# Late conditioning sections in a two-layer diffusion backbone: half of each one scaled by ScalarE and added up by GpSimd during the attention

## The chip, the cores and the metric

The kernel runs on one core of a Trainium2 chip. The core has TensorE (matmuls), VectorE, ScalarE and GpSimd (elementwise work), a sync engine whose queue issues transfers, and 16 DMA engines. The metric is the device time of one execution in microseconds, lower is better. All data are float32; a float32 matmul stands in the profile as two matmul instructions.

## The reference

Two layers over 512 latent tokens of width 1024, with 256 context tokens. Each layer takes six conditioning sections of width 1024 (shift, scale and gate, twice) out of one vector:

```
m = silu(c) @ ada_w[l] + ada_b[l]
sh1, sc1, g1, sh2, sc2, g2 = split(m, 6)
h  = rms_norm(x) * (1 + sc1) + sh1
x  = x + g1 * mixer(h)          # layer 0: pooling groups and 8 attention heads; layer 1: Conformer convolution
h2 = rms_norm(x) * (1 + sc2) + sh2
x  = x + g2 * experts(h2)       # 16 experts, each takes 64 tokens
```

`ada_w[l]` is 1024 x 6144: a section is a product of the vector with 1024 x 1024 weights, 4 MB. The context tokens have a conditioning vector of their own (`c_ctx`), which only the first two sections of layer 0 need. In the attention each head scores 512 queries against 768 keys (context and latents), takes a softmax, and weighs the values.

## The kernel before

Weights stream through `ring`, six slots of 2 MB (`SLOTS`), in the order of `ORDER`. Granule number g lies in slot g % 6 and is loaded once the granule six places before it is used up (`slot_free`, L497). All these loads are issued in program order by the sync engine (SP), so a load that waits holds back the ones behind it.

The program has these stages: the first four conditioning sections, input projection and pooling (`L0`); the attention, head by head; the output projection and the routing to experts; the experts of layer 0 (`mixture`, eight pairs); the convolution; the experts of layer 1. In the expert stages 2 MB granules follow each other through the same six slots. The first of them, besides two that lie ready in the ring, waits for the last head's output (`spare_free`, `o_done`).

Sections 4 to 9 are the six late ones (`LATE`). Head h of the attention (h = 0 to 5) computes section h + 4. Each section is loaded in two halves b = 0, 1 of 1024 x 512. A half lies in a slot as 8 pieces of 128 x 512, one for each k, and the vector as `cond`, 8 columns of 128. `ada_block` multiplies the pieces with `cond` in matmuls with 32 columns of weights; columns 0 to 15 hold copies of the latents' vector and 16 to 31 of the context's. Four row groups of the result hold four partial sums; ScalarE copies them to `ada_rows` (`late_rows_out`), TensorE transposes them (`late_turn`), and VectorE adds the four (`section_sum`, `section_bias`).

In one head the engines work as follows (tile qt = 0 to 3 stands for 128 queries):

- TensorE (L954): transposes of the last head's tile 2, late block b = 0, scores of tiles 0 and 1, transposes of tile 3, late block b = 1, scores of tile 2, the last head's product with the values (L931), transposes of tile 0, the first late turn, scores of tile 3, the second late turn, transposes of tile 1, the next head's queries (`project_queries`, L890), and after odd heads the next two heads' keys (L898).
- ScalarE (L1297): for each tile exp of the scores (L1305). Copies of the late rows (L1295) stand ahead of the exps of tile 0 and behind that of tile 1, the head's output (L1289) behind that of tile 2, the next queries (L1274) at the end.
- VectorE (L1686): for each tile the maximum of the scores (L1695), the bias from it, the division by the sum of the tile before (L1681, L1683), a copy of transposed tiles (L1675). The late sums stand at tile 3, and the next queries wait for the second of them (`section_summed`).
- GpSimd stages the next heads' weights (`stage_two_heads`).
- SP issues the load of half b of section h + 1 when late block b of head h is done (L628, L633). The two halves have one slot each.

Of the kernel before, what the change touches and what calls it, by code (L numbers as in the profile page):

```python
# [18 lines left out]
N = 512  # L19
# [5 lines left out]
HEADS = 8  # L25
# [185 lines left out]
def drains(engine, through):  # L211
# [12 lines left out]
         + [("ada", b) for b in range(4, 2 * EARLY)] + [("late", 0), ("late", 1), ("mixout", 0), ("mixout", 1)]  # L224
# [15 lines left out]
G_LATE = GRANULE[("late", 0)]  # L240
TWO_DMAS = set()


def arrivals(g):

    return 16 * sum(LATE if ORDER[n][0] == "late" else 1 + (n in TWO_DMAS) for n in range(g % SLOTS, g + 1, SLOTS))

# [24 lines left out]
def build(nc, x_in, c_in, ctx_in, cctx_in, ada_w, ada_b, norm1_g, norm2_g, mix_w_in, pool_w, pool_scale,  # L272
# [7 lines left out]
    with stack:  # L280
# [159 lines left out]
        edges_in, pads_set, pooled = map(sem, ("edges_in", "pads_set", "pooled"))  # L440
        cond_in, consts_in, params_in, small_in, attn_w_in = map(
# [50 lines left out]
        def _(sp):  # L492
# [4 lines left out]
            def slot_free(g):  # L497
# [4 lines left out]
                elif ORDER[before][0] == "moe1":  # L502
                    sp.wait_ge(moe_used, MOE_GRANULES + ORDER[before][1] + 1)
                elif ORDER[before][0] == "late":
                    sp.wait_ge(late_filled, 2 * LATE)
                else:
                    sp.wait_ge(filled, last_use(before) + 1)
# [17 lines left out]

            def late_slot(b):
                return slot(G_LATE + b).rearrange("p (k n) -> p k n", k=K8)

# [33 lines left out]
            for b in range(2):  # L562
                slot_free(G_LATE + b)
                sp.dma_start(late_slot(b), ada_blocks(0)[EARLY, b, :, :, :]).then_inc(slot_in[(G_LATE + b) % SLOTS], 16)
# [61 lines left out]
            for b in range(2):  # L626
                sp.wait_ge(late_filled, b + 1)
                sp.dma_start(late_slot(b), ada_blocks(0)[EARLY + 1, b, :, :, :])\  # L628
                  .then_inc(slot_in[(G_LATE + b) % SLOTS], 16)
            with sp.Fori(0, LATE - 2, 1) as s:  # L630
                for b in range(2):
                    sp.wait_ge(late_filled, 2 * s + (b + 3))
                    sp.dma_start(late_slot(b), ada_blocks(1)[s, b, :, :, :])\  # L633
                      .then_inc(slot_in[(G_LATE + b) % SLOTS], 16)
# [41 lines left out]
        def _(pe):  # L676
# [259 lines left out]
            def late_block(h, b):  # L936

                g = G_LATE + b
                pe.wait_ge(slot_in[g % SLOTS], arrivals(g) - 16 * (LATE - 1) + 16 * h)
                if b == 0:  # L940
                    pe.wait_ge(q_nope_done, h + 1)
                    pe.wait_ge(q_rope_done, h + 1)
                else:
# [1012 lines left out]
```

## Time and profile before

| | |
|---|---|
| median of 3 runs | 1548.9 us (1544.6 to 1551.72) |
| profiled execution | 1544.04 us, its span 1542.1 us |
| TensorE matmuls | 1418.3 us busy, 92% |
| VectorE, ScalarE, GpSimd | 432.8, 230.2, 70.9 us busy |
| DMA | 500.08 MB, mean 324 GB/s |
| mean granted TensorE clock | 0.984 |

The span runs from the first to the last instruction of one profiled execution. In the slices a digit is a tenth of busy time in 1/40 of the span (38.6 us). The attention lies from about 126 to 280 us, slices 4 to 8. The chain of waits follows the work back from the last instruction; whatever isn't on it could be longer without a change of the end, up to a point.

### The profile page before, as it was taken

The numbers are of one execution on the slowest core, as the hardware profiler recorded it, in microseconds if no ns is written. First come the engines' busy times: TensorE is split into PE (matmuls) and PEld (weight loads), VectorE is DVE, ScalarE is ACT, GpSimd is POOL, SyncE is SP. The second block draws the span as 40 slices with busy tenths as digits, with TensorE's granted clock in tenths as the row PEclk, the third lists the DMA queues.
The fourth block names the chain that finished last, engine by engine and source line by source line (L and its number), as shares of the span: only waits on it lengthen the run. The fifth ranks groups of instructions, "written<-read, shape, count | busy, mean of one in ns | idle before, by whom it ended". The sixth has DMA issues, their size and how long they took to land.

```text
span 1542.1 us, 15155 instructions
## 1 busy us (share of the span) xinstructions
PE 1418.3 (92%) x5813; PEld 586.7 (38%) x5813; DVE 432.8 (28%) x884; ACT 230.2 (15%) x469; POOL 70.9 (5%) x155
## 2 busy tenths in 40 slices
PE   5999999988999989899989999997999898999996
PEld 3544555443333332332324444453433333323322
DVE  2234667341111121111214323524012211111113
ACT  3223333111010100010003112121101000100001
POOL 1001000000000000000000300001000000000001
PEclk9999999999999999999999999998999999999999
DMA  9736683259999999999999004229999999999995
GB/s 358 263 134 235 227 300 154 82 222 382 426 400 428 427 428 428 427 428 428 421 419 365 5 0 164 95 90 348 429 415 412 428 428 428 428 429 428 423 421 218
DMA packets 77233, 500.08 MB, mean 324 GB/s; under 512 B 7752, under 2 KB 8799, under 8 KB 48766
## 3 DMA queue, kind: packets, MB, share of 16 engines
q1 hardware_dynamic: 71502, 484.10, 76.9%
q0 software_dynamic: 2304, 8.39, 1.4%
q10 hardware_dynamic: 3376, 6.86, 1.2%
q8 instruction: 38, 0.62, 0.2%
q14 instruction: 13, 0.11, 0.0%
HBM read 493.03 MB, written 6.31 MB: 324 GB/s over the span
## 4 chain that ended last, share of the span: by engine, by line
PE 66%; DMA 25%; DVE 5%; issue 1%; SPq 1%; ACT 1%; POOL 0%; POOLq 0%; DVEq 0%; ACTq 0%
PE PS L1039 28%; DMA ring<-in_exp_wg_dram 11%; DMA ring<-in_exp_wu_dram 9%; PE PS L837 7%; PE PS L1071 5%; PE PS L710 4%; PE PS L868 4%; DMA ring<-in_exp_wd_dram 3%; PE PS L681 3%; PE PS L910 3%; PE PS L693 2%; PE PS L766 2%; PE PS L762 2%; PE PS L931 1%; PE PS L852 1%
## 5 line engine op out<-in xcount | busy, mean ns | idle before, releaser
L1039 PE MATMUL PS<-ring,arena 128*64 128x512 f32 x2880 | 666.7, 601 | 43.3 <-DMA ring<-in_exp_wg_dram 19.1
L1039 PEld LDWEIGHTS PS<-ring,arena 128*64 128x64 f32 x2880 | 220.7, 138 | 458.1 <-issue 417.2
L1741 DVE TENSOR_TENSOR x<-x,PS 128x512 f32<-128x512 f32 x128 | 87.9, 687 | 465.7 <-PE PS L1071 465.7
L1071 PE MATMUL PS<-arena 128*128 128x512 f32 x256 | 141.5, 641 | 3.7 <-DVE arena L1768 3.2
L837 PE MATMUL PS<-ring,hT 128*128 128x512 f32 x256 | 113.9, 600 | 0.0
L1352 ACT ACTIVATE arena<-PS 128x512 f32<-128x512 f32 x32 | 17.4, 594 | 462.3 <-PE PS L1039 462.3
L1768 DVE SCALAR_TENSOR_TENSOR arena<-PS,arena,g_row 128x512 f32<-128x512 f32 x32 | 22.5, 746 | 218.3 <-PE PS L1039 218.3
L1071 PEld LDWEIGHTS PS<-arena 128*128 128x128 f32 x256 | 38.3, 188 | 105.1 <-issue 96.9
L681 PE MATMUL PS<-ident,arena 128*128 128x128 f32 (+4 forms) x393 | 54.1, 277 | 21.9 <-DVE arena L1759 18.0
L837 PEld LDWEIGHTS PS<-ring,hT 128*128 128x128 f32 x256 | 48.7, 192 | 59.8 <-issue 59.1
L1354 ACT ACTIVATE arena<-PS 128x512 f32<-128x512 f32 x16 | 9.6, 597 | 340.8 <-PE PS L681 340.8
L681 PEld LDWEIGHTS PS<-ident,arena 128*128 128x128 f32 (+4 forms) x393 | 44.4, 159 | 39.1 <-DVE arena L1759 22.3
L710 PE MATMUL PS<-ring,hT 128*128 128x512 f32 x128 | 56.7, 594 | 1.1 <-ACT hT L1289 1.1
L868 PE MATMUL PS<-ring,hT 128*128 128x512 f32 x128 | 56.4, 594 | 0.0
L693 PE MATMUL PS<-ring,cond 128*32 128x512 f32 x384 | 49.3, 642 | 2.1 <-DMA ring<-in_ada_w_dram 1.3
L681 PE MATMUL PS<-ident,xn 128*128 128x128 f32 x212 | 30.7, 291 | 15.2 <-DVE xn L1389 13.7
L1873 POOL DMA_INDIRECT xn<-xn_rows,token_at x16 | 15.3, 959 | 554.9 <-PE PS L681 516.6
L681 PEld LDWEIGHTS PS<-ident,xn 128*128 128x128 f32 x212 | 28.6, 188 | 29.1 <-issue 24.5
L1695 DVE TENSOR_REDUCE arena<-PS 128x1 f32<-128x768 f32 x32 | 30.6, 956 | 28.6 <-PE PS L910 27.4
L1305 ACT ACTIVATE arena<-PS,arena 128x768 f32<-128x768 f32 x32 | 28.9, 902 | 62.0 <-PE PS L681 33.3
L1128 ACT ACTIVATE xn<-x 128x1024 f32<-128x1024 f32 x20 | 21.1, 1057 | 108.6 <-DVE x L1422 60.2
L1759 DVE TENSOR_TENSOR arena<-arena,PS 128x512 f32<-128x512 f32 x32 | 20.4, 680 | 57.0 <-PE PS L1039 57.0
(183 smaller groups left out, 1077.6 us busy)
## 6 DMA issues: line engine op xcount, KB each, us to landing
ring<-in_exp_wg_dram SPq DMA_DIRECT2D x62, 2048.0 KB, 16.0
ring<-in_exp_wd_dram SPq DMA_DIRECT2D x62, 2048.0 KB, 19.8
ring<-in_exp_wu_dram SPq DMA_DIRECT2D x56, 2048.0 KB, 17.8
ring<-in_ada_w_dram SPq DMA_DIRECT2D x24, 2048.0 KB, 10.1
ring<-in_conv_w_pw_dram SPq DMA_DIRECT2D x6, 2048.0 KB, 19.6
hT<-in_exp_wu_dram SPq DMA_DIRECT2D x4, 2048.0 KB, 15.2
ring<-in_mix_w_out_dram SPq DMA_DIRECT2D x2, 2048.0 KB, 18.9
arena<-in_exp_wu_dram SPq DMA_DIRECT2D x2, 2048.0 KB, 7.8
```

Of the source, the lines that this page charges most:

```text
L681: return nc.tensor.transpose(o, i, ident[0:rows, 0:rows])
L693: last = nc.tensor.matmul(PS[r:r + 32, bank, :], cond[:, k, :], w[:, k, :], start=k < 4, stop=k >= 4)
L710: last = nc.tensor.matmul(PS[:, bank_of(n)[0], :], catT[:, k, t * 128:(t + 1) * 128], w, start=k == 0, stop=k == K8 - 1)
L762: last = nc.tensor.matmul(B, w, hT[:, k, :], start=k == 0, stop=k == K8 - 1)
L766: last = nc.tensor.matmul(B[:, 0:b - a], h, w, start=k == 0, stop=k == K8 - 1)
L837: last = nc.tensor.matmul(B, hT[:, k, t * 128:(t + 1) * 128], w[:, k, :], start=k == 0, stop=k == K8 - 1)
L868: last = nc.tensor.matmul(B, hT[:, k, t * 128:(t + 1) * 128], w, start=k == 0, stop=k == K8 - 1)
L910: last = nc.tensor.matmul(S[qt % 2][:, a:b], qT[:, qt * 128:(qt + 1) * 128], keys[odd][:, a:b], start=True, stop=True)
L1039: last = nc.tensor.matmul(PS[64 * e:64 * e + 64, bank + half, :], lhs[:, k, 64 * e:64 * e + 64], w[e][:, half * N:(half + 1) * N], start=k ...
L1071: nc.tensor.matmul(PS[:, 6 + i % 2, :], hot[:, (i // 2) * 128:(i // 2 + 1) * 128], y_rows[:, (i % 2) * N:(i % 2 + 1) * N], start=True, sto ...
L1695: v.reduce_max(maxima[:, qt:qt + 1], S[qt % 2][:, 0:768], AX.X).then_inc(max_step, 1)
L1741: v.tensor_tensor(part, part, PS[:, 6 + i % 2, :], ALU.add).then_inc(scat_added, 1)
```

## The change

Half b = 1 of a late section is no longer multiplied by TensorE. ScalarE multiplies each of its 8 pieces by the vector's column for that k, in place in the ring slot (`scale_late`), two pieces behind each exp of the head before; the pieces of section 4 are scaled before the first queries. GpSimd adds the 8 pieces up in 7 steps into `ada_rows[:, 1]` (`add_late`), between the stagings. The same late turns transpose the rows, and VectorE adds over all 128 partitions' values (`section_total`, 512 values in and 4 out, where `section_sum` took 32 in and 8 out). So that this sum is right for the half that TensorE computes too, `cond` is cleared and holds each vector in one column only, and the context's column is cleared before the attention.

Half b = 1 now has two slots that take turns (granules late 1 and late 2), half b = 0 has one. All loads of late sections stand in one loop, half 0 ahead of half 1 for each section. Half 0 of section number h waits for late block h - 1, half 1 for the sum of section h - 2. The granules behind them move by one slot. The loops over heads of ScalarE and GpSimd are written out.

```
-         + [("ada", b) for b in range(4, 2 * EARLY)] + [("late", 0), ("late", 1), ("mixout", 0), ("mixout", 1)]
+         + [("ada", b) for b in range(4, 2 * EARLY)] + [("late", 0), ("late", 1), ("late", 2), ("mixout", 0), ("mixout", 1)]
...
+LATE_STEPS = K8 - 1
...
+LATE_LOADS = (LATE, LATE // 2, LATE // 2)
...
-    return 16 * sum(LATE if ORDER[n][0] == "late" else 1 + (n in TWO_DMAS) for n in range(g % SLOTS, g + 1, SLOTS))
+    return 16 * sum(LATE_LOADS[ORDER[n][1]] if ORDER[n][0] == "late" else 1 + (n in TWO_DMAS) for n in range(g % SLOTS, g + 1, SLOTS))
...
+        cond_cleared, late_cond, late_scaled, late_sum = map(sem, ("cond_cleared", "late_cond", "late_scaled", "late_sum"))
...
+                elif ORDER[before] == ("late", 0):
+                    sp.wait_ge(late_filled, LATE)
...
-                    sp.wait_ge(late_filled, 2 * LATE)
+                    sp.wait_ge(late_sum, LATE_STEPS * (LATE - 2 + ORDER[before][1]))
...
-            def late_slot(b):
-                return slot(G_LATE + b).rearrange("p (k n) -> p k n", k=K8)
...
-            for b in range(2):
-                slot_free(G_LATE + b)
-                sp.dma_start(late_slot(b), ada_blocks(0)[EARLY, b, :, :, :]).then_inc(slot_in[(G_LATE + b) % SLOTS], 16)
...
-            for b in range(2):
-                sp.wait_ge(late_filled, b + 1)
-                sp.dma_start(late_slot(b), ada_blocks(0)[EARLY + 1, b, :, :, :])\
-                  .then_inc(slot_in[(G_LATE + b) % SLOTS], 16)
-            with sp.Fori(0, LATE - 2, 1) as s:
+            for h in range(LATE):
                 for b in range(2):
-                    sp.wait_ge(late_filled, 2 * s + (b + 3))
-                    sp.dma_start(late_slot(b), ada_blocks(1)[s, b, :, :, :])\
-                      .then_inc(slot_in[(G_LATE + b) % SLOTS], 16)
+                    g = G_LATE + b * (1 + h % 2)
+                    if h < 1 + b:
+                        slot_free(g)
+                    elif b:
+                        sp.wait_ge(late_sum, LATE_STEPS * (h - 1))
+                    else:
+                        sp.wait_ge(late_filled, h)
+                    l, s = divmod(EARLY + h, SECTIONS // 2)
+                    sp.dma_start(slot(g).rearrange("p (k n) -> p k n", k=K8), ada_blocks(l)[s, b, :, :, :])\
+                      .then_inc(slot_in[g % SLOTS], 16)
...
-            def late_block(h, b):
-                g = G_LATE + b
+            def late_block(h):
+                g = G_LATE
                 pe.wait_ge(slot_in[g % SLOTS], arrivals(g) - 16 * (LATE - 1) + 16 * h)
-                if b == 0:
-                    pe.wait_ge(q_nope_done, h + 1)
-                    pe.wait_ge(q_rope_done, h + 1)
-                else:
-                    pe.wait_ge(late_rows, 2 * h + 1)
+                pe.wait_ge(late_cond, 1)
+                pe.wait_ge(q_nope_done, h + 1)
+                pe.wait_ge(q_rope_done, h + 1)
...
-                    pe.wait_ge(late_rows, 2 * h + 2)
+                    pe.wait_ge(late_rows, h + 1)
+                    pe.wait_ge(late_sum, LATE_STEPS * h + LATE_STEPS)
...
             def head(h, odd, first, more, late):
...
-                    late_block(h, 0)
+                    late_block(h)
...
-                if late:
-                    late_block(h, 1)
...
+            act_e.wait_ge(cond_cleared, 1)
...
-                sc.activation(cond[:, :, 16 * v:16 * v + 16], cond_raw[:, v, :].unsqueeze(2).to_broadcast([128, K8, 16]),
-                              ACT.Silu).then_inc(cond_ready, 1)
+                sc.activation(cond[:, :, 16 * v:16 * v + 1], cond_raw[:, v, :].unsqueeze(2), ACT.Silu).then_inc(cond_ready, 1)
...
-            def late_rows_out(h, b):
-                act_e.wait_ge(late_filled, 2 * h + b + 1)
-                sc.activation(ada_rows[:, b, :], PS[:, 7, :], ACT.Copy).then_inc(late_rows, 1)
-            def head(j, odd, first, more, late):
+            def late_rows_out(h):
+                act_e.wait_ge(late_filled, h + 1)
+                sc.activation(ada_rows[:, 0, :], PS[:, 7, :], ACT.Copy).then_inc(late_rows, 1)
+            def scale_late(j, odd, k0, k1):
+                g = G_LATE + 1 + odd
+                if k0 == 0:
+                    act_e.wait_ge(slot_in[g % SLOTS], 16 * j + (arrivals(g) - 16 * (LATE // 2 - 1)))
+                for k in range(k0, k1):
+                    w = slot(g)[:, k * N:(k + 1) * N]
+                    sc.activation(w, w, ACT.Copy, scale=cond[:, k, 0:1]).then_inc(late_scaled, 1)
+            def head(j, odd, first, more, late, ahead):
...
                 for qt in range(T):
...
-                        late_rows_out(h, 0)
+                        late_rows_out(h)
...
-                    if late and qt == 1:
-                        late_rows_out(h, 1)
+                    if ahead:
+                        scale_late(*((j + 1, 0) if odd else (j, 1)), 2 * qt, 2 * qt + 2)
                     if qt == 2 and not first:
                         output(*((j, 0) if odd else (j - 1, 1)))
...
-            def two_heads(j, first=False, more=True):
-                head(j, 0, first, True, more)
-                head(j, 1, False, more, more)
+            def two_heads(j, first=False, more=True, last_late=False):
+                head(j, 0, first, True, more, more)
+                head(j, 1, False, more, more, more and not last_late)
...
+            scale_late(0, 0, 0, K8)
...
-            with act_e.Fori(1, HEADS // 2 - 1, 1) as j:
-                two_heads(j)
+            two_heads(1)
+            two_heads(2, last_late=True)
...
-            def section_bias(n):
-                return v.tensor_tensor(section_cols(n), section_cols(n),
-                                       bias_flat[:, bass.ds(n * K8, K8)].unsqueeze(1).to_broadcast([128, 2, K8]), ALU.add)
+            def section_bias(n, samples=2):
+                part = section_cols(n)[:, 0:samples, :]
+                return v.tensor_tensor(part, part, bias_flat[:, bass.ds(n * K8, K8)].unsqueeze(1)
+                                       .to_broadcast([128, samples, K8]), ALU.add)
+            def section_total(n, half, B):
+                return v.tensor_reduce(section_cols(n)[:, 0, 4 * half:4 * half + 4],
+                                       B.rearrange("p (k n) -> p k n", k=4), AX.X, ALU.add)
...
+            v.memset(cond[:, :, :], 0.0).then_inc(cond_cleared, 1)
...
                 for qt in range(T):
                     if late and qt == 3:
...
-                        section_sum(h + EARLY, 0, PS[:, 7, :]).then_inc(late_summed, 1)
+                        section_total(h + EARLY, 0, PS[:, 7, :]).then_inc(late_summed, 1)
...
                     if late and qt == 3:
...
-                        section_sum(h + EARLY, 1, PS[:, 7, :]).then_inc(section_summed, 1)
+                        section_total(h + EARLY, 1, PS[:, 7, :]).then_inc(section_summed, 1)
...
                     if late and qt == 3:
...
-                        section_bias(h + EARLY).then_inc(late_added, 1)
+                        section_bias(h + EARLY, 1).then_inc(late_added, 1)
...
+            v.memset(cond[:, :, 16:17], 0.0).then_inc(late_cond, 1)
...
-            def stage_two_heads(j):
-                stage_queries(2 * j)
-                if not isinstance(j, int) or j > 0:
+            def add_late(h):
+                g = G_LATE + 1 + h % 2
+                acc = ada_rows[:, 1, :]
+                pool.wait_ge(late_scaled, K8 * h + K8)
+                if h == 0:
+                    pool.wait_ge(filled, place(0, "sel", 3, 1) + 1)
+                else:
+                    pool.wait_ge(late_turned, 2 * h)
+                for k in range(1, K8):
+                    if k > 1:
+                        pool.wait_ge(late_sum, LATE_STEPS * h + k - 1)
+                    p.tensor_tensor(acc, slot(g)[:, 0:N] if k == 1 else acc, slot(g)[:, k * N:(k + 1) * N], ALU.add)\
+                     .then_inc(late_sum, 1)
+            def stage_keys(j):
+                if j > 0:
...
                 p.tensor_copy(wk_stage.rearrange("p (a b) -> p a b", a=2),
...
-                if isinstance(j, int):
-                    pool.wait_ge(drained_v, drains("V", len(L0) - 1))
-                    pool.wait_ge(drained_s, drains("S", len(L0) - 1))
-                stage_values(2 * j, 0)
-                stage_queries(2 * j + 1)
-                stage_values(2 * j + 1, 1)
...
-            stage_two_heads(0)
-            with pool.Fori(1, HEADS // 2, 1) as j:
-                stage_two_heads(j)
+            stage_queries(0)
+            stage_keys(0)
+            pool.wait_ge(drained_v, drains("V", len(L0) - 1))
+            pool.wait_ge(drained_s, drains("S", len(L0) - 1))
+            for h in range(HEADS):
+                if h:
+                    stage_queries(h)
+                    if h % 2 == 0:
+                        stage_keys(h // 2)
+                stage_values(h, h % 2)
+                if h < LATE:
+                    add_late(h)
```

## Rows read from the trace of the kernel before

**Rows 1.** The page, busy tenths in 40 slices of the span: TensorE and DMA.
```profile
PE   5999999988999989899989999997999898999996
DMA  9736683259999999999999004229999999999995
```

**Rows 2.** Sync queue in order of time: start, us, issue.
```profile
280.57 0.34 SPq L575 DMA_DIRECT2D arena<-in_exp_wu_dram  x1
```

**Rows 3.** Chain of waits in order of time, attention: start, us, engine, tile, line, count.
```profile
126.56 1.85 PE PS L693 x16
...
141.54 1.92 PE PS L693 x16
...
161.01 1.85 PE PS L693 x16
...
176.49 1.97 PE PS L890 x4
...
179.42 1.93 PE PS L693 x16
...
217.29 1.92 PE PS L693 x16
```

**Rows 4.** Timeline of head 1: start, us, instructions, idle before them.
```profile
146.18 0.90 ACT L1305 ACTIVATE arena<-PS,arena 128x768 f32<-128x768 f32 x1 [2.05 <-DVE arena L1697]
...
147.47 0.90 ACT L1305 ACTIVATE arena<-PS,arena 128x768 f32<-128x768 f32 x1 [0.30 <-DVE arena L1697]
...
148.69 1.56 PE L910 MATMUL PS<-xn,arena 128*128 128x512 f32 x4
...
154.07 1.46 PE L910 MATMUL PS<-xn,arena 128*128 128x512 f32 x4
...
155.56 0.96 DVE L1695 TENSOR_REDUCE arena<-PS 128x1 f32<-128x768 f32 x1 [0.68 <-PE PS L910]
...
157.10 1.96 PE L890 MATMUL PS<-arena 128*128 128x512 f32 x4 [0.49 <-DVE cols L1406]
```

**Rows 5.** Groups by line and shape, whole span: count, busy us, mean ns, idle before.
```profile
L1180 ACT ACTIVATE ada_rows<-ada_rows 128x512 f32<-128x512 f32 x8 | 5.0, 630 | 85.6 <-DVE ada_rows L1609 85.6
L1194 ACT ACTIVATE hT<-hT,cols,amp 128x512 f32<-128x512 f32 x4 | 2.9, 800 | 0.0
L1888 POOL TENSOR_TENSOR x<-x,arena 128x1024 f32<-128x1024 f32 x4 | 9.7, 2463 | 0.1
L1406 DVE TENSOR_REDUCE cols<-PS 128x8 f32<-128x32 f32 x14 | 2.7, 190 | 29.2 <-PE PS L681 29.2
L1675 DVE COPY xn<-PS 128x768 f32<-128x768 f32 x32 | 30.5, 954 | 17.0 <-PE PS L681 16.8
L1683 DVE TENSOR_SCALAR arena<-arena 128x768 f32<-128x768 f32 x32 | 20.0, 624 | 1.1
```

**Rows 6.** Issues of conditioning loads, and groups with KB and us to landing.
```profile
100.28 0.54 SPq L515 DMA_DIRECT2D ring<-in_ada_w_dram  x1
100.86 0.67 SPq L564 DMA_DIRECT2D ring<-in_ada_w_dram  x1
163.07 0.54 SPq L633 DMA_DIRECT2D ring<-in_ada_w_dram  x1
...
ring<-in_ada_w_dram SPq DMA_DIRECT2D x1, 2048.0 KB, 8.6
ring<-in_ada_w_dram SPq DMA_DIRECT2D x1, 2048.0 KB, 14.0
```

**Rows 7.** Busy time in stretches: length, PE, PEld, DVE, ACT, POOL, granted clock, DMA share, GB/s.
```profile
350.00:351.00 1.00, 0.00 (x0) 0.00 (x0) 0.90 (x5) 0.00 (x0) 0.00 (x0) 1.00 0.89 377
353.00:354.00 1.00, 1.00 (x7) 0.90 (x5) 0.19 (x1) 0.00 (x0) 0.14 (x1) 0.50 0.96 410
356.00:357.00 1.00, 1.00 (x4) 0.39 (x3) 0.00 (x0) 0.00 (x0) 0.30 (x1) 0.81 0.68 176
```

**Rows 8.** Timeline before the first queries: ScalarE's last instruction ahead of the change's scaling.
```profile
121.55 0.84 ACT L1322 ACTIVATE xn<-arena 64x768 f32<-64x768 f32 x1
```

## The prediction

> **What bounds the kernel now.** I read the row of slices first [rows 1]. Two stages differ: up to about slice 8 (some 300 us) TensorE is busy and the DMA engines come and go; in the expert stages the DMA row stands at 9. The change touches only the attention (126 to 280 us). So two questions: what sets the attention's length, and does a shift of its end reach the end of the program? For the second: the first expert load that waits for the attention's outputs is issued at 280.57 [rows 2], right behind them, and the slices around it show the DMA engines nearly idle. Nothing behind it runs on a clock of its own, so I take a shift of the attention one to one to the end.
>
> For the first, the chain of waits in order of time [rows 3] is almost all TensorE: a head with late conditioning starts with its first late block, and those of heads 0 and 5 start at 126.56 and 217.29: 90.73 us for five heads, 18.1 each. The timeline of head 1 [rows 4] gives the inner times, counted from its late block at 141.54: exp of tile 0 at +4.6, exp of tile 1 at +5.9, scores of tile 3 at +12.5, their maximum at +14.0, next projection of queries at +15.6, next head 19.5 after the last.
>
> **What is taken away.** One late block of 16 matmuls per head, 1.85 us on the chain [rows 3]. Scores of tile 2, which stood behind it at 148.69, then wait for exp of tile 0 (146.18, plus 0.90 and a handoff, estimated 1.05 together: 147.23) [rows 4]. So at most 1.46 of the 1.85 us comes back. The 0.60 us copy of its rows on ScalarE goes too.
>
> **Section sums on VectorE.** They now read 512 values a partition instead of 32. A small one takes 0.19 [rows 5], the maximum over 768 values 0.96 [rows 4]; by proportion 0.64, so +0.46 (bounds 0 and +0.77). The first is hidden before the maximum of tile 3 in a head as it runs now, the second stands before the projection. Net gain of a head without other trouble: 1.46 - 0.46 = 1.0 us. The two clears of the conditioning tile are some 0.1 us beside loads: nothing.
>
> **GpSimd.** Seven adds of 128x512. An add of 128x1024 takes 2.46 [rows 5]; half is 1.25, with a wait each some 9.2 us in a head (bounds: nothing, and 7 x 2.46 = 17.2). They start when the previous head's second turn is done and the last scaling is in, at about -1, and must be ready for the late turn at about +11; they are. Queued behind them is the staging of the next queries, about 1 us, wanted at the head's end: hidden too. The Trainium skill, page "SBUF — State Buffer", section "SBUF: two separate sides", speaks against this move: GpSimd and a VectorE operation that takes the shared port pair lock each other out for a whole instruction. No row of before shows both at once. By it an add could wait for a division (0.62 [rows 5]) or the reverse by 1.25; the two divisions in that stretch have some 3 us of room, and the sum stays.
>
> **The load order, the term that decides.** ScalarE scales section h+1 during head h, two pieces after each exp, and it first waits for the slot of that section, in order, ahead of exp of tile 1. When does that slot arrive? The sync queue issues for each section first the half for TensorE, which waits until late block h has run (it refills the one slot G_LATE), and behind it the half for ScalarE. That half's own wait is over early, but it stands in the queue behind the other. So both halves of section h+1 are issued only after head h's late block, and ScalarE wants the second of them 5 us later. Before, a half was wanted a whole head later.
>
> Price: late block to issue is 163.07 - 161.01 = 2.06 [rows 3, 6]. Two such loads back to back stand in the trace at 100.28 and 100.86: they land 8.6 and 14.0 us after their own issue [rows 6]. So the second lands at 2.06 + 0.58 + 14.0 = +16.6 in the head, against +5.9, where exp of tile 1 runs now. From there:
> - two scalings: with a scale column a 128x512 from SBUF takes 0.80 with bias and scale, 0.63 with neither [rows 5]; I take 0.73: 1.46, to +18.1.
> - exp of tile 1, 0.90 and a handoff: scores of tile 3 may start at +19.15 instead of +12.5.
> - TensorE has then stood for 8 us. In the trace, after an idle stretch from 350 to 352, the granted clock was 0.50 at 353 although the engine worked, and 0.81 at 356 [rows 7]: a return takes some 3 to 4 us. So tile 3's scores run at 1.2 GHz, 1.4 us later at their end: to the maximum 1.49 [rows 4] + 1.4, at +22.0.
> - VectorE meanwhile: division 0.77 with its reciprocal, copy 0.95 [rows 5], section sum 0.64, from +19.1: +21.5, no later.
> - maximum to projection is 1.54 now [rows 4], plus 0.46 for the second sum: projection at +24.0.
> - From projection to next late block: 2.93 in even heads (176.49 to 179.42), 3.91 in odd ones (157.10 to 161.01) [rows 3, 4]: +26.9 and +27.9.
> - ScalarE after +18.1: exps of tiles 1, 2, 3 (1.0 each), six scalings (4.4), output copies (0.76), then the queries' copy (0.6): done at +26.9. In even heads it is as late as TensorE: 27.0.
>
> The stall swallows the 1.46 us. Five heads (0 to 4) prepare a following section: 3 x 27.0 + 2 x 27.9 = 136.8 against 90.73: **+46.1 us**. Bounds per head: scaling at 0.63 or 0.80 moves it by 0.8 at most, the clock by 0 to 3.
>
> On the clock the Trainium skill says, page "TensorE: Matmul & The Clock Gate", section "Part 1: The HAM clock gate", that TensorE falls to 1.2 GHz when idle and must work for a while to come back. The trace agrees (0.50 at 353). By the rule alone each of the five holes costs; without any fall the sum would be 1 us less (0.5 in each odd head; in even ones ScalarE holds the end).
>
> **Start and last head.** Before the first queries ScalarE now scales eight pieces: it is free at 121.55 + 0.84 = 122.39 [rows 8], + 5.84 + 0.6 for the queries = 128.8, late block 0 at 128.9 instead of 126.56 [rows 3]: **+2.3** (bounds 1.5 and 3). The slot is there long before. Head 5 prepares nothing: **-1.0**. Unrolled loops, the extra ring slot and the moved load of the last slot: the same number of loads (two of output weights, two of conditioning, two of experts) is in before the attention ends, and the slots move by one; nothing.
>
> **Sum.** 46.1 + 2.3 - 1.0 = +47.4. The profiled execution took 1544.0 (span 1542.1, 1.9 around it): 1591.4. The median of the runs is 1548.9, 4.9 above it; on that level 1596.3. I forecast **1596 us**, slower; its own range is 1585 to 1606. 0.5% (7.7 us) is about what a measurement of this kernel can tell from no change.
>
> **Rivals.**
> - *Not slower: the half arrives in time.* If the second half did not queue behind the first, or landed by +5.9, ScalarE would not stall. Per head 1.0 x 6 = 6.0 gained, 2.3 lost at the start: 1545; with both sums hidden as well and the start too, 1.46 x 6 = 8.8: 1540. For it: the waits of that half alone are over early, and the DMA row has holes. Against: the queue is in order, and even a lone load takes 8.6 [rows 6]. Chance 0.09, of which 0.03 at 1540.
> - *The two halves share the engines and land together at a lone load's time*, 8.6 after issue: +11.2 instead of +16.6, 5.4 x 5 = 27 less: 1569. Against: 14.0 in [rows 6]. It decides by the DMA's rate. Chance 0.07.
> - *The clock stays down past the projection.* Then both turns and the projection (1.96 [rows 4]) double: +3 per head, 15 more: 1611. For it: the fall at 353; against: the return by 356 [rows 7]. The page on the clock gate is the one above. Chance 0.08.
> - *GpSimd becomes the bound.* If port conflicts made an add over some 2.9 us, the late turn would wait for it, and with it the rest of the head: at 3.4 us an add (23.8 a head) about 4 more in six heads: 1620. Against: 2.46 for twice the size. The page on SBUF is for it. Chance 0.03.
> - The forecast: 0.73.
>
> Slower by over 0.5%: 0.73 + 0.07 + 0.08 + 0.03, 0.91; within 0.5%, 0.06; faster, 0.03. The range from 1575 to 1613 leaves out the first two rivals and the last, 0.19.
>
> **What would show it.** In the profile after: the wait ahead of the first scaling of each head put down to the DMA into the ring, 9 to 11 us, five times; both loads of a section issued within 0.6 us, some 2 us after the late block; late blocks 27 us apart for heads 0 to 5 and under 19 after; scores of tile 3 at about +19; a granted clock below 1 inside these heads; ScalarE's scaling at 0.7 each; GpSimd's adds at 1.2 to 1.3 with no one waiting for them; everything from the attention's end shifted by one amount. The prediction is wrong if exp of tile 1 stays at +6, or if an expert stage is shorter by what the attention lost.

## The result, and the profile after

The changed kernel takes 1594.6 us (median of 4, 1591.34 to 1597.92) against 1548.9 before: ratio 1.0297, interval 1.0277 to 1.0316. Its profiled execution spans 1589.3 us, 47.2 more than before. Of all the runs below one, of e8, stood apart (1721.7 us at a granted clock of 0.838) and is left out of its median.

The page's slices (TensorE, granted clock and DMA; a slice is 39.7 us here) answer to [rows 1]:

```profile
PE   5996677997999998999998999997999999988996
PEclk9998889998999999999999999999999999999998
DMA  9643529027999999999999502317999999999994
```

TensorE's digits fall to 6 and 7 in slices 4 to 7, and the clock to 8 in slices 4 to 6. Behind them the pattern is that of before, one slice later. The sync queue shows the same at the attention's end, against 280.57 in [rows 2]:

```profile
324.05 0.34 SPq L576 DMA_DIRECT2D arena<-in_exp_wu_dram  x1
```

That is 43.5 of the 47.2 us. The chain of waits, in order of time (start, us, what), answers to [rows 3]:

```profile
128.47 1.96 PE PS L697 x16
130.45 0.54 SPq L637
...
131.03 13.64 DMA ring<-in_ada_w_dram
144.70 0.03 ACT ring L1305
...
155.06 1.96 PE PS L697 x16
157.04 0.54 SPq L637
...
157.62 13.20 DMA ring<-in_ada_w_dram
...
183.93 0.59 POOL ada_rows L1877
184.52 13.13 DMA ring<-in_ada_w_dram
...
210.44 13.56 DMA ring<-in_ada_w_dram
...
237.69 13.36 DMA ring<-in_ada_w_dram
...
261.39 1.92 PE PS L697 x16
```

Before, this stretch was TensorE's. Now each head holds 13.1 to 13.6 us of one transfer, half a conditioning section on its way to the ring, issued when the late block ends. Late blocks 0 and 5 are 132.92 us apart; they were 90.73. Ahead of the last three transfers the chain names GpSimd's adds, since these loads wait for a sum. But that sum had long been ready: the add that the transfer at 184.52 waits for ended at 164.16, and the sync queue issued the pair at 183.94, just behind late block 2 (181.95, 1.92 long). So it is the late block that releases these loads too.

Head 0 in order of time (start, us, instructions, idle before them) answers to [rows 4]:

```profile
134.15 1.56 PE L914 MATMUL PS<-arena 128*128 128x512 f32 x4 [0.97 <-ACT arena L1315]
...
144.70 1.33 ACT L1305 ACTIVATE ring<-ring,cond 128x512 f32<-128x512 f32 x2 [10.60 <-DMA ring<-in_ada_w_dram]
145.94 0.88 ACT L1315 ACTIVATE arena<-PS,arena 128x768 f32<-128x768 f32 x1
...
146.96 2.93 PE L914 MATMUL PS<-arena 128*128 128x512 f32 x4 [8.57 <-ACT arena L1315]
...
149.92 0.96 DVE L1713 TENSOR_REDUCE arena<-PS 128x1 f32<-128x768 f32 x1 [0.70 <-PE PS L914]
...
151.82 2.21 PE L894 MATMUL PS<-arena 128*128 128x512 f32 x4
...
152.12 0.90 ACT L1315 ACTIVATE arena<-PS,arena 128x768 f32<-128x768 f32 x1 [1.88 <-PE PS L685]
```

ScalarE stands 10.60 us ahead of its first scaling. Exp of tile 1, in order behind it, starts at 145.94. TensorE has had nothing to do for 8.57 us when tile 3's scores start (5.3 to 6.4 us in heads 1 to 4), and they take 2.93 us in all five heads where they took 1.46. Exp of tile 3, the last row, then waits 1.88 us for TensorE's transposes. Who waited for whom between 128 and 270 us (us in total, times, longest):

```profile
ACT ring L1305 <- DMA ring<-in_ada_w_dram: 51.7, 5, 10.6
DVE arena L1699 <- ACT arena L1315: 45.9, 5, 10.1
...
PE PS L914 <- ACT arena L1315: 34.6, 11, 8.6
```

There are five waits, one for each section that is prepared. The other two rows are mostly their echo. The two issues of head 0 and each one's time to landing answer to [rows 6]:

```profile
130.45 0.54 SPq L637 DMA_DIRECT2D ring<-in_ada_w_dram  x1
131.03 0.67 SPq L637 DMA_DIRECT2D ring<-in_ada_w_dram  x1
...
ring<-in_ada_w_dram SPq DMA_DIRECT2D x1, 2048.0 KB, 8.9
ring<-in_ada_w_dram SPq DMA_DIRECT2D x1, 2048.0 KB, 13.6
```

The new groups, and VectorE's divisions, from 120 to 310 us (count, busy, mean ns, idle before) answer to [rows 5]:

```profile
L1701 DVE TENSOR_SCALAR arena<-arena 128x768 f32<-128x768 f32 x32 | 24.9, 778 | 1.1
L1427 DVE TENSOR_REDUCE cols<-PS 128x512 f32 (+1 forms) x12 | 8.2, 686 | 0.3
...
L1305 ACT ACTIVATE ring<-ring,cond 128x512 f32<-128x512 f32 x48 | 31.5, 711 | 51.7 <-DMA ring<-in_ada_w_dram 51.7
...
L1877 POOL TENSOR_TENSOR ada_rows<-ada_rows,ring 128x512 f32<-128x512 f32 x36 | 48.0, 1333 | 2.8
```

### The profile page after: what moved, and what is told of

The parts are those of the page before. It is cut to its first block, busy times and chain, and to the rows that moved or that the text cites. A ratio compares the mean times of both kernels' runs of the same rounds, so it can differ in the third digit from the quotient of the medians.

```text
span 1589.3 us, 14928 instructions
## 1 busy us (share of the span) xinstructions
PE 1422.4 (89%) x5717; PEld 591.8 (37%) x5717; DVE 443.5 (28%) x886; ACT 254.9 (16%) x511; POOL 126.5 (8%) x197
## 4 chain that ended last, share of the span: by engine, by line
PE 61%; DMA 27%; DVE 4%; ACT 2%; issue 2%; SPq 1%; POOL 1%; POOLq 0%; ACTq 0%; DVEq 0%
PE PS L1040 29%; DMA ring<-in_exp_wg_dram 10%; DMA ring<-in_exp_wu_dram 9%; PE PS L841 7%; DMA ring<-in_ada_w_dram 5%; PE PS L1072 5%; PE PS L714 3%; PE PS L872 3%; PE PS L685 3%; PE PS L770 2%; PE PS L766 2%; DMA ring<-in_exp_wd_dram 2%; PE PS L914 2%; PE PS L856 1%; PE PS L849 1%
## 5 line engine op out<-in xcount | busy, mean ns | idle before, releaser
L841 PE MATMUL PS<-ring,hT 128*128 128x512 f32 x256 | 112.2, 593 | 0.0
L1826 POOL TENSOR_SCALAR ms<-ssq 128x1 f32<-128x1 f32 x22 | 6.4, 290 | 550.2 <-ACT xn L1129 549.4
L914 PE MATMUL PS<-arena 128*128 128x512 f32 (+1 forms) x64 | 27.8, 573 | 23.1 <-ACT arena L1315 21.9
L1877 POOL TENSOR_TENSOR ada_rows<-ada_rows,ring 128x512 f32<-128x512 f32 x36 | 48.0, 1333 | 2.8
L697 PE MATMUL PS<-ring,cond 128*32 128x512 f32 x288 | 37.9, 659 | 3.7 <-ACT arena L1275 2.4
L1305 ACT ACTIVATE ring<-ring,cond 128x512 f32<-128x512 f32 x48 | 31.5, 711 | 51.7 <-DMA ring<-in_ada_w_dram 51.7
## 6 DMA issues: line engine op xcount, KB each, us to landing
ring<-in_ada_w_dram SPq DMA_DIRECT2D x24, 2048.0 KB, 13.3
```

What stands on the lines that cost most here:

```text
L697: last = nc.tensor.matmul(PS[r:r + 32, bank, :], cond[:, k, :], w[:, k, :], start=k < 4, stop=k >= 4)
L841: last = nc.tensor.matmul(B, hT[:, k, t * 128:(t + 1) * 128], w[:, k, :], start=k == 0, stop=k == K8 - 1)
L914: last = nc.tensor.matmul(S[qt % 2][:, a:b], qT[:, qt * 128:(qt + 1) * 128], keys[odd][:, a:b], start=True, stop=True)
L1877: p.tensor_tensor(acc, slot(g)[:, 0:N] if k == 1 else acc, slot(g)[:, k * N:(k + 1) * N], ALU.add)\
```

## The experiments

All are edits of the changed kernel. A time with a plus sign is counted in us from the start of the head's late block. For each profile the table has the starts of late blocks 0, 1 and 5, the gap between blocks 1 and 5 over four (full heads, without the start), the issue of the first expert load behind the attention, and the median time. In the later measurements the kernel before had medians of 1547.7 to 1548.1 us; the ratios and intervals compare with those.

| kernel | block 0 | block 1 | block 5 | per head | attention's end | time |
|---|---|---|---|---|---|---|
| before | 126.56 | 141.54 | 217.29 | 18.94 | 280.57 | 1548.9 |
| after | 128.47 | 155.06 | 261.39 | 26.58 | 324.05 | 1594.6 |
| e1, ScalarE's half loaded a head ahead | 130.14 | 147.11 | 221.40 | 18.57 | 284.73 | 1552.6 |
| e2, halves swapped | 129.16 | 150.29 | 232.23 | 20.49 | 294.88 | 1563.2 |
| e3, scaling at the head's end | 128.86 | 150.95 | 241.08 | 22.53 | 306.22 | 1574.8 |
| e4, e1 without scaling and adds | 127.10 | 142.37 | 215.97 | 18.40 | 278.61 | 1545.6 |
| e5, e1 with short sums | 128.71 | 144.18 | 216.09 | 17.98 | 278.24 | 1548.0 |
| e6, e1 with section 4 on TensorE | 127.37 | 143.42 | 218.81 | 18.85 | 282.14 | 1550.1 |
| e7, e4 with short sums | 127.48 | 141.72 | 213.32 | 17.90 | 275.46 | 1545.1 (one run) |
| e8, e1 without adds | 129.45 | 144.72 | 218.31 | 18.40 | 280.95 | 1547.0 |
| e9, e1, scaling of one value | 127.24 | 142.52 | 217.04 | 18.63 | 279.67 | 1546.5 |
| e10, after with the clock held | 127.93 | 153.05 | 260.42 | 26.84 | 323.05 | 1591.9 |

**1. Only the load order.** One loop over pairs puts ScalarE's half of section h + 1 ahead of TensorE's half of section h:

```
-            for h in range(LATE):
-                for b in range(2):
...
+            for h, b in [(0, 0), (0, 1), (1, 1)] + [(h + i, i) for h in range(1, LATE) for i in range(2) if h + i < LATE]:
...
+                    sp.wait_ge(late_sum, LATE_STEPS * (h - 1))
```

> The changed kernel with one edit: in the sync queue the load of ScalarE's half of section h+1 stands ahead of TensorE's half of section h, so it is issued once section h-1's pieces are added up, a head earlier. Theory (the queue order decides): no wait ahead of the first scaling, exp of tile 1 back at about +6 to +7, late blocks 17 to 18 us apart instead of 26.6. Span about 1542.1 + 1.9 (start) - 6 x 1.0 = 1538, time 1540 to 1546, some 45 us under the changed kernel. Rival (ScalarE's 5.3 us of scaling a head, or GpSimd's 9.4 us of adds, hold the head up): late blocks 21 us or more apart and at least 1560.

1552.6 us (1550.41 to 1554.76), 42 less than the changed kernel, 1.003 of before (1.0018 to 1.0042). In its head 1 (late block at 147.11) no wait for a DMA is left:

```profile
151.74 0.90 ACT L1314 ACTIVATE arena<-PS,arena 128x768 f32<-128x768 f32 x1 [2.05 <-DVE arena L1714]
...
152.63 1.32 ACT L1304 ACTIVATE ring<-ring,cond 128x512 f32<-128x512 f32 x2
...
153.85 0.89 ACT L1314 ACTIVATE arena<-PS,arena 128x768 f32<-128x768 f32 x1
```

Exp of tile 1 is at +6.7 with the scaling ahead of it. ScalarE and GpSimd do the same work as in the changed kernel, so that work is not what cost 45 us; the order of two loads in a queue was nearly all of it. But the kernel isn't faster than before, and it is 7 to 13 us above what I expected of it. Its start, in order of time:

```profile
124.39 5.01 ACT L1304 ACTIVATE ring<-ring,cond 128x512 f32<-128x512 f32 x8 [0.84 <-DMA gates<-cols]
...
130.14 3.41 PE L696 MATMUL PS<-ring,cond 128*32 128x512 f32 x16 [2.42 <-ACT arena L1274]
```

TensorE waited 2.42 us for the queries behind the eight scalings, and the block that followed took 3.41 instead of 1.92 us, at the lower clock (granted 0.50 from 130 to 133). With the wait for a gate's transfer (0.84) this execution lost some 5 us before head 1, where the changed kernel's profile lost 1.9 up to its late block.

**2. The halves of a section swapped.** Both still wait for the late block.

```
+            for h, b in [(0, 0), (0, 1)] + [(h, b) for h in range(1, LATE) for b in (1, 0)]:
...
+                if h:
+                    sp.wait_ge(late_filled, h)
```

> The changed kernel with the two loads of a section swapped: both still issued after the late block, but ScalarE's half first. Theory (the end of the transfer sets the head): the half lands 8.5 to 9 us after issue instead of 13.4 after, that is 5.2 to 5.6 us earlier in the head; exp of tile 1 ends near +13 where TensorE comes to tile 3's scores at +11.7, so late blocks about 20.8 us apart, 5.8 less in five heads: about 1566. Rival (any stall of ScalarE costs, whatever its end, by the shrunken clock of TensorE for example): less than 15 us gained. Rival (stalls that end before +12 are hidden): a gap near 17.5 and 1545.

1563.2 us (1560.47 to 1565.71). ScalarE in head 0 (late block at 129.16):

```profile
140.17 1.33 ACT L1306 ACTIVATE ring<-ring,cond 128x512 f32<-128x512 f32 x2 [5.39 <-DMA ring<-in_ada_w_dram]
```

The wait ends at +11.0 instead of +16.2. The five heads take 103.1 us, 20.6 each, where 20.8 were expected: 5.2 us earlier in the head make a head 6.0 us shorter. The theory that the end of the transfer sets the head holds, and the one by which any stall costs alike falls. That a head gains more than the 5.2 us fits the clock: tile 3's scores take 2.93 us here in head 0 only and 1.56 in the other four. Part of a stall is free: in head 1 exp of tile 1 stands at +11.9 where e1 has +6.7, 5.2 us later, and a full head is 1.9 us longer than in e1.

**3. The wait behind the last exp.**

```
-                    if ahead:
-                        scale_late(*((j + 1, 0) if odd else (j, 1)), 2 * qt, 2 * qt + 2)
...
+                    if ahead and qt == 3:
+                        scale_late(*((j + 1, 0) if odd else (j, 1)), 0, K8)
```

> The changed kernel with its load order, but ScalarE does the eight scalings of the next section after the last exp of the head, not two after each exp. Theory (the wait costs through exp of tile 1, which stands behind it): the wait now ends at +15.6 with nothing but the queries behind it; scaling 5.3 us from there, queries at +21.6, late blocks 21.7 us apart, five heads 108 to 109 instead of 132.9: about 1570. Rival (the landing sets the head wherever the wait stands): no gain, 1590 to 1596.

1574.8 us (1569.84 to 1575.23), 20 less than the changed kernel with the same late loads. Five heads take 112.2 us, 3 to 4 more than expected: late blocks wait up to 6.4 us for the queries, and some then run at the lower clock (0.50 in the one shown), which the expectation left out:

```profile
150.95 3.64 PE L697 MATMUL PS<-ring,cond 128*32 128x512 f32 x16 [6.36 <-ACT arena L1275]
```

So what stands behind the wait in ScalarE's order sets about half of its price here, 20 of 42 us.

**4. Neither scaling nor adds**, with the load order of e1; half of each section is left out. The loads that waited for a sum wait for the late turns in its place.

```
-                for k in range(k0, k1):
...
-                if h < LATE:
-                    add_late(h)
...
-                    pe.wait_ge(late_sum, LATE_STEPS * h + LATE_STEPS)
```

> The first kernel of this call (half a head ahead) without the scalings and the adds: half of each late section is left out. What the removed late block is worth at most. Theory: no start cost, 1.0 us a head less than before: span 1536, time 1538 to 1543, within 2 us and the start's 1.9 us of the first kernel. Rival (scaling and adds cost time even where they don't wait): the first kernel is 5 us or more slower than this.

1545.6 us, ratio to before 0.9987 (0.9972 to 1.0002). Even with half of the late work gone the time shows no gain that can be told from none; by the profile a head is 0.54 us shorter, not 1.0. And e1 is 7.0 us slower than this, by its expectation the mark of the rival: scaling and adds cost time even where they don't wait for a load. Of that, 4.7 us are lost by late block 1 (147.11 against 142.37).

**5. Short sums.**

```
-                                       B.rearrange("p (k n) -> p k n", k=4), AX.X, ALU.add)
+                                       B.rearrange("p (k n) -> p k n", k=4)[:, :, 0:8], AX.X, ALU.add)
```

> The kernel with the half loaded a head ahead, whose section sums read 8 of each 128 values (32 in all, not 512): part of each sum is left out, so that the reading costs what it did before the change. Theory (the longer sums take back part of the block: they cost 0.5 us each, and the second stands before the projection): late blocks 0.5 us closer in six heads, attention end 3 us earlier than 284.73, time 1549 to 1550. Rival (the block's other 1.4 us were hidden behind exp and the weighing anyway): no change, 1552.6.

1548.0 us (1545.32 to 1550.96); per head 17.98 against 18.57, so the long sums cost 0.6 us a head. The theory holds. The time moved 4.6 us, more than six heads of it, part of that at the start.

**6. Section 4 on TensorE**, so that nothing is scaled ahead of the first queries.

```
+                if first:
+                    first_second()
...
-            scale_late(0, 0, 0, K8)
...
-                if h < LATE:
+                if 0 < h < LATE:
                     add_late(h)
```

> The kernel with the half loaded a head ahead, but section 4 wholly on TensorE as before the change, so that nothing is scaled before the first queries and nothing added in head 0; sections 5 to 9 as changed. Theory (what the repaired kernel still lacks is its start: late block 0 at 130.14 and run at 1.2 GHz against 126.56): late block 0 back at 126.6 with 1.9 us of length, attention end 279 to 280 against 280.57 before and 284.73; time 1545 to 1549, no change from before that can be measured. Rival (scaling and adds in heads 1 to 5 cost the rest): 1551 or more.

1550.1 us, ratio 1.0013 (1.0001 to 1.0025). It is the best complete version of the change, and lies between the two expectations. Late block 0 is at 127.37 and back at 1.92 us, but heads 2 and 3 took 19.1 and 19.5 us and the attention ended 1.6 us later than before; which of the scalings, adds and sums makes these two longer wasn't separated. No complete version beats the kernel before.

**7. Neither, and short sums.** The sums of e5 in the kernel of e4.

> The kernel without scalings and adds (half of each section left out), and with the short sums too. The most that the removed block can be worth. Theory (sums take 0.5 a head): late blocks of heads 1 to 5 another 0.5 us closer than 18.4 in the mean, attention end at 275.5 instead of 278.61. Rival: at 278.6, then something else stands where the block stood.

The attention ends at 275.46, as expected to 0.1 us. A head takes 17.90 us against 18.94 before: the block alone is worth 1.04 us, and the long sums take 0.50 back (e4 less e7).

**8. Scaling without adds.** The adds and TensorE's wait for them go as in e4, the scaling stays; slots wait for the scaling and the turns.

> The kernel with the half loaded a head ahead, with ScalarE's scaling and without GpSimd's adds: the second rows of each late section stay what they were. In that kernel the first expert load of the attention's end came 137.6 us after head 1's late block, without scaling and adds 136.2. If the adds cost the 1.4 us (divisions on VectorE held up to 1.6 us beside them): 136.2 here, no division over 0.7 us, time about 1551. If the scaling costs it: 137.6.

From late block 1 to the first expert load it is 280.95 - 144.72 = 136.2 us, as without both: beside the scaling, the adds cost the 1.4 us. VectorE's divisions (shortest, median, longest ns) between 126 and 290 us, first in e1, then here:

```profile
L1700 DVE TENSOR_SCALAR arena<-arena x32: 619/621/1642, 137.6 to 270.0; 128x768 f32<-128x768 f32 x32
```

```profile
L1701 DVE TENSOR_SCALAR arena<-arena x32: 619/620/653, 135.4 to 266.2; 128x768 f32<-128x768 f32 x32
```

Count and median are the same; only with GpSimd's adds in the kernel do single ones take up to 1.64 us, and the 32 together 26.7 us instead of 19.9. The time is 1547.0 us, 4 less than expected, and the same as before within the interval (ratio 1.0003, 0.9984 to 1.0022).

**9. Adds without scaling.** Each scaling covers one value; the rest stays unscaled.

```
-                    w = slot(g)[:, k * N:(k + 1) * N]
+                    w = slot(g)[:, k * N:k * N + 1]
```

> The kernel with the half loaded a head ahead, with the adds, and each of ScalarE's scalings over one value of a piece instead of 512 (the rest stays unscaled). The adds can start earlier. If the adds cost the 1.4 us: 137.6 from head 1's late block to the first expert load behind the attention. At the start ScalarE needs 8 x 0.2 us, so late block 0 within 1 us of where it was before the change and TensorE at full clock: time 1547 to 1549, 4 us under the kernel with both.

From block 1 to the load it is 137.15 us, between the two: without the scaling the adds cost 0.9 us, not 1.4, and with short sums (e5 against e7) both together cost 0.3 us in that stretch (134.06 against 133.74). So the adds' price depends on what runs beside them, and each of these figures is from one profile. Late block 0 is at 127.24; the time is 1546.5 us, just under what was expected.

**10. The changed kernel with its clock held.**

```
+                if h < LATE - 1:
+                    warm(18)
                 score(h, odd, 3)
```

(`warm` is that many 128x256 matmuls into a free half of a bank; ScalarE's copy of the bank's other half waits for them. TensorE's loop over heads is written out.)

> The changed kernel, its load order untouched, with 18 matmuls of 128x256 that nobody reads between the first late turn and the scores of tile 3 in heads 0 to 4, so that TensorE works in the hole. Forecast's theory (the fall of the granted clock lengthens tile 3's scores by 1.4 us, of which 0.5 to 1.5 us a head is on the path): granted clock 1.00 in the heads, scores of tile 3 at 1.46 us instead of 2.93, late blocks 1 to 1.5 us closer than 26.6, time 5 to 7 us less: 1588 to 1590. Rival (the clock is hidden behind the division, the copy and the sum on VectorE): same time, 1594 to 1596.

1591.9 us (1589.88 to 1594.8), 2.7 less than the changed kernel, between theory and rival. The two sets of four runs overlap, so this difference alone isn't clear of noise. The expectation also asked more of the clock than the prediction did, which had it at 1 us in all. Shown are the changed kernel's granted clock (last but two) in head 0's hole and behind it, then this kernel's over the attention:

```profile
145.00:146.00 1.00, 0.00 (x0) 0.00 (x0) 0.00 (x0) 1.00 (x3) 0.00 (x0) 0.50 0.00 0
147.00:148.00 1.00, 1.00 (x2) 0.48 (x3) 0.96 (x3) 1.00 (x2) 0.00 (x0) 0.50 0.00 0
...
153.00:154.00 1.00, 1.00 (x5) 0.46 (x4) 0.34 (x1) 1.00 (x4) 0.00 (x0) 1.00 0.00 0
```

```profile
128.00:324.00 196.00, 177.35 (x906) 114.05 (x907) 103.09 (x189) 76.13 (x142) 65.50 (x87) 1.00 0.47 172
```

Tile 3's scores take 1.45 to 1.56 us again. Late blocks are hardly closer (132.49 us for five heads against 132.92), for two reasons. ScalarE's five waits for the ring came to 55.1 us against 51.7; why its transfers landed later is open. And the extra matmuls themselves hold TensorE up in heads 1 to 3. In head 2:

```profile
191.47 7.94 PE L984 MATMUL PS<-x,ones 128*128 128x256 f32 x36
195.57 1.33 ACT L1313 ACTIVATE ring<-ring,cond 128x512 f32<-128x512 f32 x2 [10.18 <-DMA ring<-in_ada_w_dram]
...
199.24 1.45 PE L914 MATMUL PS<-arena 128*128 128x512 f32 x4
```

Tile 3's scores start 3.67 us after ScalarE's wait has ended, without any wait of their own, where in heads 0 and 4 they start 2.26 us after it. Over heads 1 to 3 that is 2.6 us more. From the end of ScalarE's wait to the next late block, the five heads are 3.8 us shorter than in the changed kernel (49.3 against 53.1), of which 1.2 and 0.9 us lie in heads 0 and 4, where the extra matmuls hold nothing up. So by these rows the clock costs 3.8 us or more in five heads; an estimate that adds the 2.6 back is 6.4.

## Why the prediction was right, step by step

The forecast was 1596 us and +47.4; measured 1594.6, spans +47.2. The same sum, term by term:

| term | forecast | measured |
|---|---|---|
| start, to late block 0 | +2.3 | +1.9 |
| five heads | +46.1 | +42.2 |
| from late block 5 to the attention's end | -1.0 | -0.6 |
| behind the attention | 0 | +3.7 |

By the medians the change is 45.7 us, by the spans 47.2. That the sum met the spans to 0.2 us is luck: it had 3.9 us too much in the five heads, and 3.7 us came behind the attention that it didn't have.

- *Load order decides*: shown. e1 changes it alone and takes 42 us back.
- *Late block to landing +16.6*: +16.2 in head 0 (1.98 + 0.58 + 13.6). The pair at 100.28 in [rows 6] priced it well.
- *Scalings 1.46, to exp at +18.1*: they follow each other every 0.62 (1.24 from the first to exp), +17.5. The mean length of 0.71 of one scaling holds its overlap with the next.
- *Tile 3's scores at +19.15, maximum at +22.0, projection at +24.0*: +18.5, +21.5, +23.4.
- *Heads of 27.0 and 27.9*: 26.6, 26.9, 25.9, 27.2, 26.3. Most of the 3.9 us by which the five were over-forecast is the landing (15.7 to 16.2 in the five heads) and the scaling.
- *In even heads ScalarE holds the end*: the end is ScalarE's, but not by the sum's working. The sum had it busy without a break from +18.1 to +26.9. In head 0 its row ends at +26.4, with 1.88 us of waiting for TensorE's transposes in it, and less work: the six scalings take 4.0 us, not 4.4, and the first head has no output to copy. The two nearly cancel.
- *The clock falls in the holes*: right as a fact, too cheap as a price. The granted clock is 0.50 in head 0's hole and at tile 3's scores, and 1.00 at 153 (the rows under 10). The Trainium skill, page "TensorE: Matmul & The Clock Gate", section "Part 1: The HAM clock gate", has TensorE at half clock when idle and at full clock again after sustained work; the trace agrees. The price was put at 1 us in all, and at nothing in even heads. By the rows of e10 it is 3.8 us or more, and 1.2 and 0.9 us of it lie in the even heads 0 and 4; by time it is 2.7 us and not clear of noise. What was wrong is that ScalarE's row was taken as independent of TensorE's clock.
- *GpSimd hidden*: in the changed kernel it is, save 1.34 us of wait in head 0's first late turn. The add took 1.33 us in the mean, 1.27 in the median; forecast 1.25. The Trainium skill, page "SBUF — State Buffer", section "SBUF: two separate sides", describes a lock by which a GpSimd instruction and a VectorE operation that takes the shared port pair hold each other up for a whole instruction. e1 and e8 agree with it: single divisions take up to 1.64 us in the kernel with the adds and at most 0.65 without. That it is this lock, and not another contention between the two, no run here shows. The waits of TensorE's weight loads that the profile puts down to divisions are 1.5 us in the changed kernel as in the one before, and 2.4 in e1, where the adds cost 0.2 us a head (18.57 against 18.40 in e8).
- *Sum 0.64*: 0.69, and +0.5 on the path (e4 less e7). The proportion took all of an instruction's time as growing with its values. A line through the two rows that the prediction had (0.19 at 32 values, 0.96 at 768) gives 0.69 at 512.
- *1.46 us of the block come back, 1.0 net*: **this step was mis-sized**. It was hidden under the stall, so the forecast didn't suffer. Measured are 1.04 gross (e7) and 0.54 net (e4). I moved one instruction (tile 2's scores) forward and took the whole row behind it to move along. In head 1 of e7 these scores do start 1.48 us earlier than before (+5.67 against +7.15), but the product with the values behind them only 1.01 earlier (+7.62 against +8.63), since it then waits 0.39 us for VectorE's copy of transposed tiles.
- *Everything behind shifts alike*: about. From the first expert load to the end of the span it was 1261.5 us before and 1265.3 after. In the ten edits, which have the changed kernel's code there, it was 1261.5 (e3), 1261.9 (e4, e8), 1264.6 (e2), 1264.8 (e9, e10), 1265.2 (e5), 1265.6 (e6), 1267.3 (e1) and 1267.5 (e7). The 3.7 us lie within that scatter; I didn't allow for it, and no run shows another cause.

The rivals: the late half in time is what e1 made true, and it gives 1552.6, not the 1545 or 1540 of the forecast, since the start, the adds and the sums were priced too low there and the removed block too high. "Both land at a lone load's time" is nearly e2 (1563.2, forecast 1569). The clock did stay down longer than I took it to: in head 0 to 152, so the late turns and transposes behind tile 3's scores ran slowly (1.06 and 1.49 us against 0.60 and 0.82) and the projection in part (2.21 against 1.96). In heads 1 to 4 the projection took its usual 1.95 or 1.96, so the rival's 3 us a head did not come. GpSimd's adds at 1.33 us are far from the 2.9 us at which they would bind.

## What to carry to other kernels

A queue with waits is a program. For each load ask which wait stands ahead of it, not only what it waits for itself: here a half whose own condition had been met some 20 us earlier (164.16 for the one issued at 184.5) stood behind one that can't be issued before the late block is done.

Issue a load early enough for the first instruction that others need and that stands behind its wait in the waiting engine's order. Here the second of two 2 MB halves took 13.1 to 13.6 us from its issue, and exp of tile 1 was needed 6 us into the head.

Before work is moved off the busiest engine, take it out altogether and time that. Here this moved the attention's end by 2.0 us (e4, with the long sums) or 5.1 us (e7, with short ones), and neither showed clearly in the time. In e1 the same long sums together with ScalarE's scaling at the start and GpSimd's adds put the end 4.2 us later than before.

## What the runs showed of the hardware beyond that

- Two 2 MB loads issued 0.58 us apart landed 8.4 to 8.9 and 13.1 to 13.6 us after their issue in the changed kernel, so the second landed about 5.3 us behind the first (139.4 and 144.7 in head 0). With the halves swapped (e2) it was 8.4 to 9.0 and 13.3 to 13.6 in the first four pairs.
- A GpSimd add of 128x512 took 1.27 us in the median and 1.66 at most (changed kernel; mean 1.33). A VectorE division of 128x768 took 0.62 us in the median, and up to 1.64 in e1 and 1.70 in the changed kernel with these adds; without them (e8) the longest was 0.65.
- A wait of TensorE of 2.42 us was followed by a block of 3.41 us instead of 1.92, at a granted clock of 0.50 (e1), while waits of 1.60 (after), 2.39 (e5) and 2.41 us (e8) were followed by one at 1.92. What decides between them no run here shows.
